# Two decoder layers with convolution, latent attention and mixture of experts on one core: router, roots, embedding matmuls, pieces loaded ahead, rotary keys and taps rearranged

## The chip, the cores and the metric

The kernel runs on one core of one Trainium2 chip, all in fp32, as one program with a hand-written order of instructions on each engine: PE (TensorE), DVE (VectorE), ACT (ScalarE), POOL (GpSimd) and SP (SyncE, which here only starts transfers). The metric is the time of one execution on the device in microseconds. Three executions of the kernel before were timed, and one more was profiled.

## The reference, cut to what matters

One inference step runs two layers for 256 prompt tokens and 8 sample tokens with the same weights. The width is 1024. Layer 0 mixes tokens by a causal convolution of 31 taps, layer 1 by latent attention with a paged cache: each of the 8 samples has 8 pages of 128 keys. Each page holds a compressed latent of 256 numbers a key and a rotary key of 32. Behind either mixer stands a mixture of 32 experts in 4 groups, and then a gated embedding.

```python
def rmsnorm(x, g):
    return x * lax.rsqrt(jnp.mean(x * x, axis=-1, keepdims=True) + EPS) * g

def conformer_conv(h, buf, w_pw1, b_pw1, w_dw, b_dw, ln_g, ln_b, w_pw2):
    u = h @ w_pw1 + b_pw1
    u = u[..., :D_CONV] * jax.nn.sigmoid(u[..., D_CONV:])
    full = jnp.concatenate([buf, u], axis=1)
    z = conv_depthwise(full, w_dw) + b_dw
    return jax.nn.silu(layernorm(z, ln_g, ln_b)) @ w_pw2, full[:, -(CONV_WIDTH - 1):]

# latent attention of the samples, keys and latents gathered by page_table
s = (einsum('bqhl,bkl->bhqk', q_lat, c_kv) + einsum('bqhr,bkr->bhqk', q_pe, k_pe)) * ATTN_SCALE
out = einsum('bhqk,bkl->bqhl', softmax(s), c_kv)

# every layer:
#   h += mixer(rmsnorm(h))
#   h += hier_moe(rmsnorm(h))
#   h += (p[i] @ W_in) * sigmoid(rmsnorm(h) @ W_gate)
```

## The kernel before, in words

**Layout.** The hidden state hT lies with the width on the partitions, in 8 chunks of 128 (KD = 8), and 264 tokens in the columns. For the choice of experts tokens lie on partitions, in three tiles of 128, 128 and 8.

**Convolution.** `expand(c)` (matmuls recorded at L483) makes one chunk of the two halves of the first projection, 8 matmuls of 128x264 for each half. DVE's `glu` and ACT's sigmoid gate it, and `shift_blocks` (L451), called by SP for two channel blocks and by ACT for the other two, copies it four times, shifted by one token each, by DMA (arena<-arena). `taps(p)` (L518 to L522, recorded at L507) convolves the chunks 2p and 2p + 1 with 128 small matmuls that use four taps at a time; DVE's `prompt_taps` (L1058) takes them out. Then follow a layer norm, pw2 with 64 matmuls of 128x264 (L483), the residual and the squares. DVE's first work is `gained` (L996), which multiplies x by a gain from the vectors.

**Router and routing.** `last_sum` (L471) ends the sum of squares over the width; the root is made on [128x264] by ACT (`root`) and DVE (`inverse_root`). `moe` (L536) begins with the router, where for each of three token tiles the tokens are the held matrix and the 36 router columns move (L544, 24 matmuls), then turns the inverse roots to columns by token (L551), makes rows of tokens by transposing (L558), multiplies the embedding `p @ W_in` (`pin`, L563 to L568, 8 chunks, of which 5 stand ahead of the count and 3 behind the ranks), and counts tokens by expert (L576) and ranks them (L582) once DVE's `route` (L1105 to L1134) has made the one-hot rows rt_M. DVE then derives a permutation of the experts by load, and windows of 64 tokens. `gather` (L602) picks tokens by one-hot matmuls.

**Experts.** Two experts make a pair. `gate_up` (L623) multiplies gate and up weights, `turn_hid` transposes, `down` (L649) multiplies the down weights, `combine` (L664) adds into hT with the gates of the tokens.

**The stream of weights.** A piece is 1 MB (128 x 2048 numbers; gate, up or down of an expert, or 1 MB of another matrix). SP issues them in the order of use into a ring of 9 slots (`NSLOT`): the slot of piece g is g mod 9, and its load waits for the last use of piece g - 9. For experts that is the whole pair's gate and up (`gate_up_done`) or down matmuls (`down_done`). `MOE_PIECES` gives the order. `expert_stream` (L1952) loads, before the permutation is known, eight ring pieces, then six pieces to places outside the ring (`ASIDE`) and the ninth ring piece. After that the number of each expert is read from the permutation (L1968), and its pieces are issued (L1942).

**Attention.** PE goes through 16 heads in a loop of 19 steps (L926 to L942). The eight samples form two batches of four, each with scores (L892), weights (L901), values (L914, L916) and output (L922). The first batch's four parts stand in steps 3, 5, 7 and 9 of the loop, the second's behind the loop. For each batch SP first reads 32 page numbers (`page_numbers`, L1923), then issues 32 transfers of cache pages (`load_cache`, L1933; 256 KB each), of which four sequences fill all buffers: those of the second batch wait for the values of the first. POOL starts the 32 key transfers of a batch (`load_kpe`, L1859; 16 KB each) in a loop of its own. After it come `so` (L949), and the output projection wo, 64 matmuls at L483.

```python
            def load_kpe(B):
                for i in range(SB):
                    with pool.Fori(0, PAGES) as n:
                        pg = pool.value_load(pages[0:1, bass.ds(n + (SB * B + i) * PAGES, 1)], min_val=0,
                                             max_val=NPOOL - 1)
                        pool.dma_start(KPT[DR * i:DR * (i + 1), bass.ds(n * PAGE, PAGE)],
```

## Time and profile before

| what | value |
|---|---|
| runs shown, median (lowest to highest) | 950.71 us (944.7 to 959.28) |
| profiled execution, its own time | 951.04 us |
| its span | 949.3 us |
| mean granted clock of PE | 0.921 |
| PE busy | 785.6 us, 83% |
| DVE, ACT, POOL busy | 34%, 22%, 6% |
| moved by DMA | 269.32 MB, 284 GB/s over the span |

The span is the time between the first and the last recorded instruction; the execution's own time is a little longer. Busy shares are means over stages that differ much: layer 0 has its convolution until about 123, pw2 until 154, the routing until 186, experts until 419 and the embedding until 453; layer 1 has attention until 610, wo until 641, routing until 670, experts until 902, then the embedding and the last norm.

### The profile page before, as it was taken

To read this page: it belongs to the slowest core of one execution; us is meant where nothing else is said; L and a number is where in the kernel's file an instruction comes from. 1 tells how busy PE (TensorE), PEld (TensorE's weight loads), DVE (VectorE), ACT (ScalarE), POOL (GpSimd) and SP (SyncE) were. 2 spreads that over 40 slices of the span, in tenths; PEclk is the share of its full clock that TensorE was granted. 3 is DMA by queue.
4 is the path that set the end of the run, shared out by engine and by line. 5 is a ranking of instruction groups with operands and counts; after the bars stand their busy time and mean duration, and the time that the engine had idled before them with its cause. 6 is when DMAs were issued, how large, how long until landed. Compare 5 with 4: busy or idle time off the path is not lost.

```text
span 949.3 us, 16693 instructions
## 1 busy us (share of the span) xinstructions
PE 785.6 (83%) x6434; PEld 569.2 (60%) x6434; DVE 321.6 (34%) x948; ACT 206.6 (22%) x490; POOL 56.2 (6%) x95
## 2 busy tenths in 40 slices
PE   5899889999777796989997685798998787878894
PEld 4767568765453464667774362587755455545683
DVE  1512333523131331255265272226232231313435
ACT  2100131621111111132135251015211110111222
POOL 3300000000000000000033232000000000000000
PEclk9989998999988988999999796799998898899997
DMA  9941826499999999974319164468699999999501
GB/s 370 368 111 51 266 76 257 164 394 408 415 417 416 415 418 415 419 317 137 129 58 348 33 222 154 164 235 314 271 401 421 414 418 417 416 415 416 220 1 46
DMA packets 59613, 269.32 MB, mean 284 GB/s; under 512 B 7312, under 2 KB 12704, under 8 KB 38416
## 3 DMA queue, kind: packets, MB, share of 16 engines
q1 hardware_dynamic: 53088, 259.31, 69.1%
q10 hardware_dynamic: 3856, 5.40, 1.9%
q0 software_dynamic: 2592, 3.54, 1.2%
q8 instruction: 53, 0.87, 0.4%
q14 instruction: 24, 0.20, 0.1%
HBM read 261.05 MB, written 2.52 MB: 278 GB/s over the span
## 4 chain that ended last, share of the span: by engine, by line
PE 49%; DMA 26%; issue 13%; POOLq 4%; DVE 4%; ACT 2%; ACTq 1%; POOL 1%; SPq 1%; DVEq 0%
DMA ring<-in_moe_w_up 22%; PE bank L623 15%; PE bank L483 13%; PE bank L602 6%; POOLq L1857 3%; PE bank L649 3%; PE bank L507 3%; PE bank L664 2%; DMA arena<-in_stateT 2%; PE bank L892 2%; DMA arena<-arena 1%; PE bank L544 1%; PE bank L558 1%; POOLq L1859 1%; POOLq L1856 1%
## 5 line engine op out<-in xcount | busy, mean ns | idle before, releaser
L623 PE MATMUL bank<-ring,arena 128*32 128x256 f32 x2048 | 148.2, 436 | 62.6 <-DMA ring<-in_moe_w_up 60.2
L623 PEld LDWEIGHTS bank<-ring,arena 128*32 128x32 f32 x2048 | 86.5, 125 | 129.9 <-issue 107.6
L483 PE MATMUL bank<-xn_sq,ring 128*128 128x264 f32 x480 | 109.8, 391 | 10.3 <-DVE xn_sq L996 10.3
L483 PE MATMUL bank<-arena,ring 128*128 128x264 f32 (+1 forms) x456 | 108.7, 399 | 6.5 <-ACT arena L1597 4.0
L483 PEld LDWEIGHTS bank<-xn_sq,ring 128*128 128x128 f32 x480 | 92.2, 193 | 27.1 <-issue 11.1
L1229 DVE TENSOR_TENSOR arena<-arena,bank 128x128 f32<-128x128 f32 x34 | 9.8, 288 | 287.7 <-ACT arena L1638 287.7
L483 PEld LDWEIGHTS bank<-arena,ring 128*128 128x128 f32 x456 | 89.8, 198 | 23.4 <-issue 7.0
L602 PEld LDWEIGHTS bank<-arena 128*128 128x128 f32 x864 | 97.9, 192 | 9.4 <-issue 9.4
L602 PE MATMUL bank<-arena 128*128 128x128 f32 (+1 forms) x864 | 101.1, 277 | 2.0 <-DVE arena L1199 2.0
L649 PE MATMUL bank<-ring,arena 128*32 128x512 f32 x512 | 65.4, 598 | 16.6 <-ACT arena L1645 16.4
L664 PE MATMUL bank<-arena 128*128 128x264 f32 (+1 forms) x288 | 70.7, 399 | 4.7 <-ACT arena L1654 4.7
L664 PEld LDWEIGHTS bank<-arena 128*128 128x128 f32 (+1 forms) x288 | 54.2, 193 | 21.3 <-ACT arena L1654 6.9
L1246 DVE TENSOR_TENSOR hT<-hT,bank 128x264 f32<-128x264 f32 x144 | 61.7, 429 | 13.5 <-PE bank L664 11.4
L1654 ACT COPY arena<-bank 64x512 f32<-64x512 f32 x68 | 39.5, 580 | 76.6 <-PE bank L649 75.8
L1638 ACT ACTIVATE arena<-bank 128x128 f32<-128x128 f32 x34 | 9.4, 278 | 165.8 <-PE bank L623 165.8
L649 PEld LDWEIGHTS bank<-ring,arena 128*32 128x32 f32 x512 | 14.9, 109 | 44.3 <-ACT arena L1645 24.3
L1859 POOL DMA_DIRECT2D arena<-in_cache_kpeT x64 | 32.1, 501 | 72.2 <-issue 72.2
L507 PE MATMUL bank<-arena 128*32 128x256 f32 x512 | 31.2, 405 | 5.8 <-DMA arena<-arena 5.8
L892 PE MATMUL bank<-arena 128*32 128x512 f32 (+1 forms) x96 | 15.6, 474 | 19.7 <-DMA arena<-in_cache_kpeT 19.7
L1569 ACT ACTIVATE xn_sq<-hT 128x264 f32<-128x264 f32 x40 | 16.1, 420 | 71.3 <-DVE hT L1000 65.7
L1630 ACT COPY arena<-bank 128x512 f32<-128x512 f32 (+1 forms) x18 | 10.1, 562 | 94.1 <-PE bank L602 94.1
L507 PEld LDWEIGHTS bank<-arena 128*32 128x32 f32 x512 | 16.9, 117 | 19.6 <-DMA arena<-arena 6.6
(243 smaller groups left out, 799.1 us busy)
## 6 DMA issues: line engine op xcount, KB each, us to landing
ring<-in_moe_w_gate SPq DMA_DIRECT2D x60, 1024.0 KB, 13.9
ring<-in_moe_w_up SPq DMA_DIRECT2D x60, 1024.0 KB, 10.8
ring<-in_moe_w_down SPq DMA_DIRECT2D x60, 1024.0 KB, 12.9
ring<-in_stream SPq DMA_DIRECT2D x35, 1024.0 KB, 14.4
ring<-in_cache_ckv SPq DMA_DIRECT2D x32, 256.0 KB, 7.4
arena<-in_moe_w_down SPq DMA_DIRECT2D x4, 1024.0 KB, 13.4
arena<-in_cache_ckv SPq DMA_DIRECT2D x16, 256.0 KB, 4.3
xn_sq<-in_cache_ckv SPq DMA_DIRECT2D x16, 256.0 KB, 6.1
```

The costliest lines, as they stand in the source:

```text
L483: t = mm(ps[:, 0:cols], lhs(k), rhs(k), start=(k == 0), stop=(k == n - 1))
L507: t = mm(ps[CG * b:CG * (b + 1), 0:TP], dg[:, c, TQ * b + q, :], shifted[p % 2][:, b, c % 2, NQ * q:NQ * q + TP], start=(q == 0), stop=(q ...
L602: t = mm(bank[k // 4][:, (k % 4) * n:(k % 4 + 1) * n], XR[:, i, k * P:(k + 1) * P], S[:, j % 2, i, 0:n], start=(i == 0), stop=(i == 2))
L623: t = mm(bank[2 + r][p0:p0 + U, 0:F].rearrange("p (c f) -> p c f", c=2), x, w[i][:, :, k * F + c * P:k * F + (c + 1) * P], start=(k == 0), ...
L649: t = mm(bank[4 + r][p0:p0 + U, :], hidT[:, r, U * (2 * i + c):U * (2 * i + c + 1)], w[i][:, c, h * 512:(h + 1) * 512], start=(c == 0), st ...
L664: mm(bank[CBANK[k % 4]][:, 0:T], O[0:n, j % 2, k * P:(k + 1) * P], gate[0:n, j % 2, :], start=True, stop=True).then_inc(s_cb, 1)
L892: t = mm(ps[HP * i:HP * (i + 1), 0:n], qlat[:, k, b, :] if k < KK else qps[:, b, :], keys, start=(k == 0), stop=(k == KK))
L1246: v.tensor_tensor(hT[:, k, :], hT[:, k, :], bank[CBANK[k % 4]][:, 0:T], ALU.add).then_inc(s_add, 1)
L1569: s.activation(sq[:, at + k, :], src[:, k, :], ACT.Square).then_inc(s_sq, 1)
L1654: s.copy(O[64 * r:64 * r + 64, j % 2, 512 * h:512 * (h + 1)], bank[4 + r][64 * h:64 * h + 64, :])\
L1857: pg = pool.value_load(pages[0:1, bass.ds(n + (SB * B + i) * PAGES, 1)], min_val=0, max_val=NPOOL - 1)
L1859: pool.dma_start(KPT[DR * i:DR * (i + 1), bass.ds(n * PAGE, PAGE)], a["cache_kpeT"][bass.ds(pg, 1)].rearrange("o p f -> p (o f)"))\
```

## The change

- **Start and other loads.** The vectors are loaded first on SP, ahead of x, instead of on ACT. The embedding inputs, router weights and router bias, which ACT issued at the start, are issued by ACT in its loop over chunks, at chunk 6. SP's shifts stand ahead of the next ring fills.
- **Taps a chunk later.** Order on PE: expand 0 to 4, taps 0, expand 5, 6, taps 1, expand 7, taps 2, means, taps 3. DVE's order follows.
- **Router.** The router weights are held and the tokens move: 8 matmuls of 36x264, six of them between the chunks of pw2 or wo, and two behind. ACT copies the logits and three matmuls transpose them.
- **Roots by token.** `token_sums` makes sums of squares by token with nine one-column matmuls, the last three squares separately; the root is then taken on [128x3] instead of [128x264], and nothing has to be turned.
- **Embedding matmuls** go from the routing to the experts' steps 3 to 6, two chunks each, into banks 6 and 7. Their weights are no piece of the ring but a load of their own behind piece 26.
- **Seventeen pieces loaded ahead**, nine in the ring and eight outside, instead of nine and six. The order at the start of `MOE_PIECES` differs.
- **Rotary keys** are issued by SP, between a batch's page numbers and its cache pages. The second sample batch stands inside the heads' loop, the first one step earlier.

```diff
-SAMPLE_AT = [3, 5, 7, 9]
+SAMPLE_AT = [[2, 4, 6, 8], [11, 13, 15, 17]]
...
-MOE_PIECES = both(0) + [(e, c) for e in (2, NSTAT) for c in range(3)]
+MOE_PIECES = both(0) + [(2, 0), (2, 1), (4, 2), (5, 2)]
...
-ASIDE = [(3, 0), (3, 1), (3, 2), (4, 2), (4, 0), (4, 1)]
+ASIDE = [(3, 0), (3, 1), (3, 2), (2, 2), (5, 0), (5, 1), (4, 0), (4, 1)]
...
+            def logits(l, norm, k):
+
+                if k == 0:
+                    open_bank(pe, ("router", l))
+                    pe.wait_ge(s_wr, 32)
+                pe.wait_ge(s_xn, KD * norm + k + 1)
+                t = mm(bank[taken["router", l][0]][0:G + E, 0:T], wr[:, l, k, :], xnT[:, k, :], start=(k == 0),
+                       stop=(k == KD - 1))
...
+            def router_tail(l, norm):
+
+                logits(l, norm, KD - 2)
+                token_sums(l, 0)
+                token_sums(l, 1)
+                logits(l, norm, KD - 1)
+                token_sums(l, 2)
+                ps = open_bank(pe, ("lg", l))
+                freed(pe, ("router", l))
+                for i, (t0, n) in enumerate(TILES):
+                    t = mm(ps[0:n, LG * i:LG * i + G + E], lgT[:, t0:t0 + n], ident[0:G + E, 0:G + E], start=True,
+                           stop=True)
...
-            for p in range(PAIRS):
-                expand(2 * p)
-                expand(2 * p + 1)
-                if p:
-                    taps(p - 1)
+            for c in range(KD):
+                expand(c)
+                if c >= 4 and c % 2 == 0:
+                    taps(c // 2 - 2)
+            taps(PAIRS - 2)
...
-            last_sum("n1")
+                if 0 < m < KD - 1:
+                    logits(0, 1, m - 1)
+            router_tail(0, 1)
...
-                pin(range(5))
...
-                pin(range(5, KD))
...
+                    if 3 <= j < 7:
+                        pin(j)
                     gate_up(b)
...
-                if i in SAMPLE_AT:
-                    (sample_scores, sample_weights, sample_values, sample_out)[SAMPLE_AT.index(i)](0)
-            sample_scores(1)
-            sample_weights(1)
-            sample_values(1)
-            sample_out(1)
+                for B in range(TS // SB):
+                    if i in SAMPLE_AT[B]:
+                        (sample_scores, sample_weights, sample_values, sample_out)[SAMPLE_AT[B].index(i)](B)
...
+            def column_root(l):
+
+                key = ("router", l)
+                ps = arrive(act, key)
+                s.copy(lgT, ps[0:G + E, 0:T]).then_inc(is_free(key), 1)
+                freed(act, ("sums", l))
+                s.activation(rcol[:], rcol[:], ACT.Sqrt).then_inc(s_rs, 1)
...
             def expert_stream(l):
 
-                for i in range(NSLOT - 1):
+                for i in range(5):
                     load_expert(l, i, MOE_PIECES[i][0])
-                arrive(sp, (("pw2" if l == 0 else "wo"), KD - 1))
-                for i in range(4):
+                arrive(sp, ("taps", KD - 1) if l == 0 else ("wo", 0))
+                for i in range(6):
                     load_aside(l, i)
+                for i in range(5, NSLOT):
+                    load_expert(l, i, MOE_PIECES[i][0])
                 arrive(sp, ("row", l, 2, 1))
-                for i in range(4, 6):
+                for i in range(6, 8):
                     load_aside(l, i)
-                load_expert(l, NSLOT - 1, MOE_PIECES[NSLOT - 1][0])
                 sp.wait_ge(s_perm, l + 1)
...
+                    if i == PIN_AT:
+                        sp.wait_ge(s_dn, NPR * l + 2)
+                        sp.wait_ge(s_gu, NPR * l + 3)
+                        sp.dma_start(aside[:, 5, :], a["pin"][l]).then_inc(s_win, 16)
+
+            sp.dma_start(vt[:], a["vectors"]).then_inc(s_vec, 16)
             sp.dma_start(hT[:], a["xT"]).then_inc(s_x, 16)
             for g in range(NSLOT):
                 fill(g)
             for p in range(PAIRS):
+                shift_blocks(sp, p, range(NQ // 2))
                 for g in range(NSLOT + 2 * p, min(NSLOT + 2 * p + 2, G_MOE0)):
                     fill(g)
-                shift_blocks(sp, p, range(NQ // 2))
...
             for B in range(TS // SB):
                 numbers = [page_numbers(SB * B + i) for i in range(SB)]
+                if B:
+                    arrive(sp, ("ss", B - 1, 1))
+                for i in range(SB):
+                    load_kpe(SB * B + i, numbers[i])
                 for i in range(SB):
                     load_cache(SB * B + i, numbers[i])
```

The new `load_kpe(b, pg)` of SP issues eight key transfers of one sample, with addresses from the page numbers already in registers.

The first place is the order of PE in the convolution, from the first half of the chunk at which the two orders part; L483 (L528 after) is the expansion, L507 (L552 after) the taps, and before it stands:

```order
L483 MATMUL bank<-xn_sq,ring 128x264 [waits bank_free0,w_in3]
L483 MATMUL bank<-xn_sq,ring 128x264 x7
L507 MATMUL bank<-arena 32x256 [waits tap_diagonals,bank_free1,shifted0]
L507 MATMUL bank<-arena 32x256 x31
L507 MATMUL bank<-arena 32x256 [waits tap_diagonals,bank_free2]
L507 MATMUL bank<-arena 32x256 x31
L483 MATMUL bank<-xn_sq,ring 128x264 [waits bank_free3,w_in4]
L483 MATMUL bank<-xn_sq,ring 128x264 x7
```

And after:

```order
L528 MATMUL bank<-xn_sq,ring 128x264 [waits bank_free0,w_in3]
L528 MATMUL bank<-xn_sq,ring 128x264 x7
L528 MATMUL bank<-xn_sq,ring 128x264 [waits bank_free1,w_in4]
L528 MATMUL bank<-xn_sq,ring 128x264 x7
L528 MATMUL bank<-xn_sq,ring 128x264 [waits bank_free2,w_in5]
L528 MATMUL bank<-xn_sq,ring 128x264 x7
L552 MATMUL bank<-arena 32x256 [waits tap_diagonals,bank_free3,shifted0]
L552 MATMUL bank<-arena 32x256 x31
L552 MATMUL bank<-arena 32x256 [waits tap_diagonals,bank_free4]
L552 MATMUL bank<-arena 32x256 x31
L528 MATMUL bank<-xn_sq,ring 128x264 [waits bank_free5,w_in4]
```

The first taps, which wait for the shifts (`shifted0`), now stand behind both halves of chunk 4 as well.

The second place is SP's order in the first expert stage, where the first pieces behind those loaded ahead are issued (a TENSOR_LOAD of permI reads an expert's number, ISA is a step on a register). Before:

```order
L1942 ISA [waits down_done]
L1942 DMA ring<-in_moe_w_gate 128x2048
L1942 DMA ring<-in_moe_w_up 128x2048 [waits gate_up_done]
L1942 DMA ring<-in_moe_w_down 128x2x1024 [waits gate_up_done]
L1942 DMA ring<-in_moe_w_down 128x2x1024 [waits down_done]
L1968 TENSOR_LOAD permI
L1968 ISA x2
L1942 ISA [waits gate_up_done]
L1942 DMA ring<-in_moe_w_gate 128x2048
L1942 DMA ring<-in_moe_w_up 128x2048 [waits gate_up_done]
```

And after:

```order
L1977 DMA ring<-in_moe_w_up 128x2048 [waits down_done]
L1977 DMA ring<-in_moe_w_down 128x2x1024 [waits down_done]
L1977 DMA ring<-in_moe_w_down 128x2x1024 [waits gate_up_done]
L2004 TENSOR_LOAD permI
L2004 ISA x2
L1977 ISA [waits gate_up_done]
L1977 DMA ring<-in_moe_w_gate 128x2048
L1977 DMA ring<-in_moe_w_up 128x2048 [waits down_done]
```

The last two rows of each are the gate and up piece of expert 8: the up piece waited for gate and up matmuls (`gate_up_done`) and now waits for down matmuls (`down_done`).

The third place is SP's order in the attention, where the page numbers (pages) of the first batch end and the transfers begin. Before:

```order
L1923 TENSOR_LOAD pages
L1923 ISA x2
L1933 ISA
L1933 DMA arena<-in_cache_ckv 128x512
L1933 ISA
L1933 DMA arena<-in_cache_ckv 128x512
```

And after:

```order
L1952 TENSOR_LOAD pages
L1952 ISA x2
L1968 ISA
L1968 DMA arena<-in_cache_kpeT 32x128
L1968 ISA
L1968 DMA arena<-in_cache_kpeT 32x128
```

After the last of 32 such key transfers the cache pages follow as before:

```order
L1968 DMA arena<-in_cache_kpeT 32x128
L1968 ISA
L1968 DMA arena<-in_cache_kpeT 32x128
L1962 ISA
L1962 DMA arena<-in_cache_ckv 128x512
L1962 ISA
L1962 DMA arena<-in_cache_ckv 128x512
```

32 transfers of keys, each with a register step, now stand between the page numbers and the first cache page.

## Rows read from the trace of the kernel before

**Rows 1.** Page, busy share by slice, in 40 slices of 23.7 us: DMA engines, then GB/s.

```profile
DMA  9941826499999999974319164468699999999501
GB/s 370 368 111 51 266 76 257 164 394 408 415 417 416 415 418 415 419 317 137 129 58 348 33 222 154 164 235 314 271 401 421 414 418 417 416 415 416 220 1 46
```

**Rows 2.** Chain of waits, first expert stage: start us, duration us, what, count.

```profile
231.63 10.70 DMA ring<-in_moe_w_up
...
377.95 11.34 DMA ring<-in_moe_w_up
```

**Rows 3.** Chain of waits, from the convolution to the first expert.

```profile
49.27 9.85 PE bank L507 x128
...
73.55 7.04 PE bank L507 x128
...
123.37 30.29 PE bank L483 x128
...
156.61 7.03 PE bank L544 x48
...
173.30 0.71 PE bank L576 x6
...
185.78 3.66 PE bank L623 x64
```

**Rows 4.** Chain of waits, attention and second routing.

```profile
525.80 1.92 DMA arena<-in_cache_kpeT
...
586.25 7.60 PE bank L892 x48
...
610.28 30.45 PE bank L483 x128
...
643.68 4.11 PE bank L544 x48
...
669.80 3.66 PE bank L623 x64
```

**Rows 5.** Timeline of PE, 48 to 50: start, us, instruction, [idle before <-releaser].

```profile
49.27 1.08 PE L507 MATMUL bank<-arena 128*32 128x256 f32 x8 [4.89 <-DMA arena<-arena]
```

**Rows 6.** Windows: a:b us, PE PEld DVE ACT POOL busy (count), PEclk, DMA share, GB/s.

```profile
54.00:55.00 1.00, 1.00 (x16) 0.50 (x12) 0.00 (x0) 0.00 (x0) 0.00 (x0) 0.57 1.06 216
158.00:159.00 1.00, 1.00 (x7) 1.00 (x6) 1.00 (x1) 0.00 (x0) 0.00 (x0) 0.50 1.02 426
220.00:226.00 6.00, 5.41 (x49) 5.17 (x47) 3.46 (x11) 0.70 (x3) 0.00 (x0) 1.00 0.94 359
```

**Rows 7.** Timeline of DVE, at the start and at the first choice of experts.

```profile
9.85 2.22 DVE L996 TENSOR_SCALAR xn_sq<-hT,vt 128x264 f32<-128x264 f32 x8 [9.85 <-DMA vt<-in_vectors]
...
169.87 0.26 DVE L1134 TENSOR_TENSOR rt_M<-rt_M 128x96 f32<-128x96 f32 x1
```

**Rows 8.** Page, DMA issues: out<-in, count, KB each, us to landing.

```profile
hT<-in_xT SPq DMA_DIRECT2D x1, 1056.0 KB, 6.1
```

**Rows 9.** Timeline of SP's DMA issues, first expert stage.

```profile
189.65 0.36 SPq L1942 DMA_DIRECT2D ring<-in_moe_w_gate  x1
...
216.50 0.34 SPq L1942 DMA_DIRECT2D ring<-in_moe_w_gate  x1
```

**Rows 10.** By line of SP's instructions: duration ns min/median/max, first to last start us.

```profile
L1923 SPq TENSOR_LOAD <-pages x64: 260/266/517, 479.3 to 532.2; - x64
...
L1933 SPq DMA_DIRECT2D arena<-in_cache_ckv x16: 345/346/369, 496.9 to 557.1; - x16
...
L451 SPq DMA_DIRECT2D arena<-arena x32: 627/628/1346, 32.6 to 102.3; - x32
```

**Rows 11.** Timeline of SP's cache page issues, both batches.

```profile
496.91 4.46 SPq L1933 DMA_DIRECT2D arena<-in_cache_ckv  x8
...
553.42 4.06 SPq L1933 DMA_DIRECT2D arena<-in_cache_ckv  x8
```

**Rows 12.** Tile of the cache pages: time from issue to landing.

```profile
DMA to landing us min/median/max: 2.6/6.2/9.9
```

250 lines of the change are left out of this document (129 added, 121 removed).

## The prediction

> **What bounds the kernel now.** I read the slices of the page first [rows 1]: the DMA engines stand at 9 in slices 9 to 17 and 30 to 37, the two expert stages, where they move 400 GB/s and more. There the weights' transfers set the time. Between them lie the convolution, two routing stages and the attention, with DMA mostly under 7. Then I followed the chain of waits. In the expert stage it is made of weight pieces that land, at 242.33 and at 389.29, 58 pieces apart [rows 2]: 2.53 us for a piece of 1 MB. In the convolution and the routing it stays on PE: taps, pw2 from 123.37, router from 156.61, count at 173.30, first expert matmul at 185.78 [rows 3]. In the attention it passes through the rotary keys' DMAs; the first batch's last one lands at 527.72 and PE starts its scores behind it at 527.96, those of the second batch at 586.25 [rows 4]. So there are six terms: what PE loses in the convolution and in each routing, how long each expert stage transfers, and when the attention's inputs land.
>
> **Convolution, -8.8 us.** PE waits 4.89 us for shifted taps before 49.27 [rows 5], and the 128 matmuls of this first pair of tap chunks take 9.85, against 7.04 for the same work at 73.55 [rows 3]. The granted clock in 54 to 55 is 0.57 with PE fully busy [rows 6]. After the change two more expansion halves (16 matmuls of 264 columns, 0.47 us each by the 64 of pw2 in 30.29 [rows 3], so 7.5 us) stand where PE waited. That covers the 4.89, and PE no longer comes to the taps out of a pause: 9.85 - 7.04 = 2.8 more. Later, tap and expansion work only change places on a PE that is busy either way; I cost that at nothing, and if a shift were late there it would be below 1 us. The start: DVE's first gained chunk waits for the vectors until 9.85 [rows 7]. They now go first on SP. x lands 6.1 us behind its issue [rows 8], which is in the first microsecond, so near 7.0, and near 7.5 with 50 KB of vectors ahead; the first weight piece follows x, at the latest 1 MB later, 2.8 us at the 370 GB/s of the first slice [rows 1]. I take 8.7, between the two: 1.1, with ends 0 and 2.3. The router's loads move later and remain hidden: they are due behind 150. Sum -4.9 - 2.8 - 1.1 = -8.8; ends -6.5 and -10.
>
> **First routing, -4.8 us.** Before, pw2's start to the first expert matmul is 185.78 - 123.37 = 62.41 [rows 3]. After, step by step. pw2 itself is 30.29, and 6 router matmuls between its chunks at 0.47 make 2.8. From pw2's end (153.66) to the one-hot rows (169.87 + 0.26 = 170.13, [rows 7]) it was 16.47. Out go the 48 narrow router matmuls, 7.03 [rows 3]; in come two wide ones, 0.95; roots on 128x3 instead of 128x264 save some 0.8 of DVE and ACT. That leaves 9.6. The count stood at 173.30, 3.2 behind its input, because PE had embedding matmuls ahead of it; they are gone, and 0.4 is left for the hand-over. Count to first expert matmul stays 12.48. Then the clock. Without the embedding matmuls PE has almost nothing while DVE chooses experts. Before, the pause of 3 us ahead of 156.61 was followed by a granted 0.50 with PE at 1.00 busy [rows 6]. For the gather and the first gate and up I take a loss of 2 us (0 to 6, the upper end being half of the 12.48). 30.29 + 2.8 + 9.6 + 0.4 + 12.48 + 2 = 57.6, so -4.8; ends -0.8 and -6.8.
>
> The Trainium skill, page "TensorE: Matmul & The Clock Gate", section "Why this matters for your kernels", says that idle gaps in the middle of a kernel give the fast clock back. It speaks against taking the embedding matmuls out of the routing. Rows 6 agree as far as they go (0.57 and 0.50 behind a gap). By the rule at its full price this term would be near -1 instead of -4.8.
>
> **Second routing, -1.9 us.** The same steps, but its narrow router matmuls took 4.11, not 7.03 [rows 3, 4], so 2.9 less is saved. From wo's start to the first expert matmul it was 59.52 [rows 4]. Ends +2 and -4.
>
> **Expert stages, +3.2 us each.** Seventeen pieces instead of fifteen are loaded ahead, and the embedding weights join behind them as a load of their own: one piece less in the stream, -2.5 at 2.53 a piece. What the embedding matmuls cost PE inside the experts lies beside transfers: PE waits there for pieces, of which single ones take 10.7 and 11.3 us to land [rows 2]. Against this stands the ring. From SP's first issue behind the permutation, 189.65, to the one that waits for the third pair's down matmuls, 216.50, it is 26.85 us [rows 9]. Before, pieces 9 to 19 of the order are issued in that time, 11 pieces or 27.9 us of data: the DMA engines stay at work, and the rate only dips to 359 GB/s in 220 to 226 [rows 6], where slices 10 to 16 have 408 to 418 [rows 1]. After, the ninth slot holds the down piece of expert 4, and piece 17, the up piece of expert 8 that reuses it, waits for those same down matmuls (the second place shown with the change). Only pieces 9 to 16 go out ahead, 8 or 20.3 us of data. The engines run dry for 26.85 - 20.3 = 6.6, against a dip worth about 1 before: +5.7. -2.5 + 5.7 = +3.2 for each layer. Ends -2.5 (no hole, if PE is earlier against the stream) and +4.
>
> **Attention, +13.4 us, the largest term.** Before, SP reads the first batch's 32 page numbers from 479.3 on [rows 10] and issues its cache pages from 496.91 [rows 11]: 17.6 us for 32, 0.55 each. Eight pages took 4.46 to issue, 0.56 each, though the DMA instruction itself is 0.346 [rows 10, 11]. POOL issues the keys beside this, by itself. After, SP issues 32 key transfers between numbers and pages (third place). No row shows a key's DMA on SP. From both sides: at worst 0.65, as the tap shifts with their 0.628 [rows 10]; at best 0.40, the bare 0.346 and small register steps, nothing overlapped. I take 0.55, the pitch of the cache pages, since that is the same instruction with a register in its address. Then the pages start at 496.9 + 17.6 = 514.5 and their issue ends at 532.1. A page lands 6.2 us behind its issue [rows 12], so the first scores begin at 538.2, not 527.96: +10.2. The products of the first batch end 25.3 us later as before (527.96 to 553.3; the issue at 553.42 waits for them, [rows 11]), at 563.5. SP meanwhile reads numbers (532.1 + 17.5 = 549.6), issues keys (567.2), then pages (584.8); the last lands at 591, where before the second scores began at 586.25: +4.7. From there to wo it was 610.28 - 586.25 = 24.0, batch two alone on PE. After, the batch stands inside the heads' loop, with a head between its steps, as the first batch did: 25.3 for its four steps, and 7.4 for the heads and outputs that remain behind. wo starts at 591 + 25.3 + 7.4 = 623.7, so +13.4. Per 0.1 us of key issue this moves by 8.8: with 0.40 it is near +4.6 (the second batch is then bound by other waits), with 0.65 it is +22.2. POOL is out of the path.
>
> The Trainium skill, page "DMA: Bandwidth & Descriptors", section "Issuing engines are not separate DMA queues", says that starting DMAs on several engines saves only sequencer time, usually small beside the transfer. The rows here disagree for small transfers: a key of 16 KB is 0.04 us of data at some 400 GB/s, and an issue on SP takes 0.55. By the rule the attention term would be about 0; the first rival has that as a mechanism of this kernel.
>
> **The sum.** The profiled execution took 951.04 us, its span is 949.3, and 1.7 lies around it; the runs' median is 950.71, so nothing is corrected. 951.04 - 8.8 - 4.8 + 3.2 + 13.4 - 1.9 + 3.2 = 955.3. I forecast 955 us, +0.5%. A measurement of this kernel can tell about 2% from no change: bounds 932 and 970.
>
> **The rivals.**
> One, faster: key issues on SP cost nothing that ends last. For it: SP idles before 479.3 and its order alone keeps the pages late; if it gets to the keys earlier than I think, or the heads between the steps cover the delay, attention comes to 0. With it go no hole in the stream (-2.5 twice), no clock loss (-6.8 and -3.9) and -9.9 in the convolution: 951.0 - 9.9 - 6.8 - 3.9 - 5 = 925. Against: the reads start with the stage, and the pages stand behind the keys in SP's order. Chance 0.16.
> Two: no hole in the stream, all else as forecast. 955.3 - 2 x 5.7 = 944. For it: the third pair's down may come earlier than 26.85, as more of its pieces are there beforehand. Chance 0.15.
> Three, slower: a key's issue on SP costs 0.65, as a shift's does. The place is SP's order before each batch's pages; attention +22.2, total 964. It passes 970 from 0.72 us a key on. For it: the key writes 32 partitions, a different form than the page. Against: the register steps are the same. Chance 0.20, of it beyond 970 0.12.
> Four: the change does not do what it says in the convolution; the shifts come equally late against the taps, since SP and ACT issue them in the same sequence, and only the start gains. 955.3 + 7.7 = 963. Against: the shifts now stand ahead of the ring's fills. Chance 0.05.
> The forecast itself has 0.44, with a range of its own of 946 to 963.
>
> **How the numbers follow.** Faster than 932 is rival one and the low tail of two, 0.20. Slower than 970 is rival three's tail and a sum of bad ends, 0.14. In between 0.66. The range of 931 to 970 leaves some 0.2 outside.
>
> **What would show it.** In the changed kernel's profile: no wait of PE for a shift, and a first pair of tap chunks of 7 us; pw2's start to the first expert matmul 57.6; some 6 us without transfers 21 to 27 us behind the first ring issue in each expert stage; 17.6 us of key issues on SP before each batch's pages; first scores 10 us later against the first page number than before; PE at a lower clock behind the routings. The forecast is wrong if the scores start where they did, if wo starts less than 5 us later against the first page number, if the stream shows no hole, or if the embedding matmuls show up as waits in the experts.

## The result, and the profile after

The changed kernel takes 969.89 us (median of 4 runs, 966.58 to 972.65) against 950.17 for the kernel before: a ratio of 1.0233, 95% interval 1.0183 to 1.0284. It is slower by 2.3%, where 0.5% and no measurable change were forecast; the interval leaves open whether it is a little more or a little less than 2%. The profiled execution took 966.58 us with a span of 964.6, the lowest of the four; against the one before (span 949.3) that is 15.3 us. The medians differ by 19.7 us; the other 4 us of it stand in no trace.

The chain of waits of the changed kernel, the rows that answer to [rows 3, 4] (start us, duration us, what, count; L528 is the old L483, L552 the taps L507, L490 the router, L621 the gather, L642 the first expert line, L927 the sample scores):

```profile
53.52 7.04 PE bank L552 x128
60.56 14.44 PE bank L528 x64
...
101.70 8.80 PE bank L552 x128
...
121.83 9.09 PE bank L528 x32
130.92 0.56 PE bank L490 x2
131.49 3.76 PE bank L528 x16
...
166.60 0.94 PE bank L597 x6
...
173.70 7.48 PE bank L621 x48
...
181.90 3.66 PE bank L642 x64
...
592.54 7.95 PE bank L927 x69
...
624.22 9.07 PE bank L528 x32
...
668.97 1.05 PE bank L597 x6
...
683.65 3.66 PE bank L642 x64
```

From such rows, and from the timeline of PE for the ends of the expert stages, one gets the stages, each from the start of its first PE work to that of the next:

| stage | before | after | forecast | measured |
|---|---|---|---|---|
| start to pw2 | 123.4 | 121.8 | -8.8 | -1.5 |
| pw2 to first expert matmul | 62.4 | 60.1 | -4.8 | -2.3 |
| experts, layer 0 | 231.1 | 234.0 | +3.2 | +3.0 |
| embedding and query inputs | 62.2 | 63.3 | 0 | +1.1 |
| attention, to wo | 131.2 | 145.0 | +13.4 | +13.8 |
| wo to first expert matmul | 59.5 | 59.4 | -1.9 | -0.1 |
| experts, layer 1 | 231.8 | 235.2 | +3.2 | +3.4 |
| embedding, last norm | 47.7 | 45.7 | 0 | -2.0 |

The two large costs, attention and expert stages, came near their forecast. What failed are the gains: 15.5 us were forecast and 3.9 came. The timeline of PE shows the convolution's part (start, us, instruction, [idle before <-releaser]):

```profile
11.09 6.83 PE L528 MATMUL bank<-xn_sq,ring 128*128 128x264 f32 x16 [11.09 <-DMA ring<-in_stream]
...
101.70 8.80 PE L552 MATMUL bank<-arena 128*32 128x256 f32 x128 [3.32 <-DMA arena<-arena]
```

PE starts 0.7 later than before (11.09 against 10.35) and needs 6.83 us for its first 16 matmul records (5.55 before). The first taps at 53.52 wait for nothing and take 7.04, as forecast; but the last ones now wait 3.32 us and take 8.80. Before, they had this row:

```profile
104.93 7.11 PE L507 MATMUL bank<-arena 128*32 128x256 f32 x128 [0.87 <-DMA arena<-arena]
```

In the middle of the changed kernel's last taps the granted clock is about half (windows, in the form of [rows 6]):

```profile
104.00:106.00 2.00, 2.00 (x25) 0.97 (x20) 0.00 (x0) 0.00 (x0) 0.00 (x0) 0.51 1.03 434
```

SP's issues in the first expert stage, and the windows around them (a:b us; busy time of PE, PEld, DVE, ACT, POOL; clock; DMA share; GB/s):

```profile
185.80 0.42 SPq L1977 DMA_DIRECT2D ring<-in_moe_w_down  x1
...
195.70 0.34 SPq L1977 DMA_DIRECT2D ring<-in_moe_w_gate  x1
212.47 0.34 SPq L1977 DMA_DIRECT2D ring<-in_moe_w_up  x1
```

```profile
190.00:206.00 16.00, 15.27 (x205) 10.64 (x197) 3.86 (x12) 3.35 (x7) 0.00 (x0) 1.00 1.02 410
206.00:214.00 8.00, 7.64 (x77) 4.73 (x73) 3.72 (x9) 1.71 (x4) 0.00 (x0) 1.00 0.39 127
214.00:230.00 16.00, 15.21 (x176) 10.94 (x169) 5.72 (x17) 2.47 (x6) 0.00 (x0) 1.00 0.98 407
```

Against [rows 9]: between a gate piece at 195.70 and its up piece at 212.47 SP issues nothing, and from 206 to 214 the DMA engines are busy for 39% of the time. That is the hole. It was forecast as 6.6 us, 5.7 more than before; 61% of 8 us is 4.9, and summed in windows of 2 us the missing share is 5.4 us, against 0.3 in the dip before. The forecast's frame was right too: 26.67 us pass from the first issue at 185.80 to the one at 212.47 (26.85 forecast), with 8 pieces ahead of the wait.

SP in the attention, against [rows 11]; then the key transfers by line (duration ns min/median/max):

```profile
497.36 16.17 SPq L1968 DMA_DIRECT2D arena<-in_cache_kpeT  x32
513.71 3.97 SPq L1962 DMA_DIRECT2D arena<-in_cache_ckv  x8
...
549.12 16.87 SPq L1968 DMA_DIRECT2D arena<-in_cache_kpeT  x32
566.17 4.54 SPq L1962 DMA_DIRECT2D arena<-in_cache_ckv  x8
```

```profile
L1968 SPq DMA_DIRECT2D arena<-in_cache_kpeT x64: 315/316/1421, 497.4 to 565.7; - x64
```

32 key issues in 16.17 us are 0.505 each, where 0.55 was taken. The pages start at 513.71; 514.5 was forecast. What PE's scores wait for has changed with it. The timeline of PE at the first scores, of the kernel before and then of the changed kernel:

```profile
527.96 1.03 PE L892 MATMUL bank<-arena 128*32 128x512 f32 x1 [10.99 <-DMA arena<-in_cache_kpeT]
```

```profile
539.67 1.03 PE L927 MATMUL bank<-arena 128*32 128x512 f32 x1 [24.82 <-DMA ring<-in_cache_ckv]
```

Before, the keys end last: POOL's loop issues one each 1.5 us (32 from 478.55 to 525.80). After, the cache pages behind the keys on SP end last.

### The profile page after: what moved, and what is told of

Same layout as the page of the kernel before. It is cut to its first block, busy times and chain, and to the rows that moved or that the text cites. A ratio compares the mean times of both kernels' runs of the same rounds, so it can differ in the third digit from the quotient of the medians.

```text
span 964.6 us, 16235 instructions
## 1 busy us (share of the span) xinstructions
PE 784.6 (81%) x6398; PEld 564.8 (59%) x6398; DVE 316.0 (33%) x946; ACT 207.6 (22%) x492; POOL 24.1 (3%) x32
## 4 chain that ended last, share of the span: by engine, by line
PE 57%; DMA 25%; SPq 8%; issue 4%; DVE 4%; ACT 1%; ACTq 1%; DVEq 0%
DMA ring<-in_moe_w_up 22%; PE bank L528 20%; PE bank L642 14%; PE bank L621 6%; SPq L1952 3%; SPq L1962 3%; PE bank L668 3%; PE bank L697 3%; SPq L1968 3%; PE bank L552 2%; PE bank L473 1%; DMA ring<-in_stream 1%; PE bank L490 1%; DMA ring<-in_cache_ckv 1%; PE bank L927 1%
## 5 line engine op out<-in xcount | busy, mean ns | idle before, releaser
L642 PE MATMUL bank<-ring,arena 128*32 128x256 f32 x1984 | 135.9, 426 | 59.9 <-DMA ring<-in_moe_w_up 57.5
L642 PEld LDWEIGHTS bank<-ring,arena 128*32 128x32 f32 x1984 | 82.6, 122 | 118.5 <-issue 94.8
L528 PE MATMUL bank<-xn_sq,ring 128*128 128x264 f32 x480 | 111.1, 394 | 11.1 <-DMA ring<-in_stream 11.1
L528 PE MATMUL bank<-arena,ring 128*128 128x264 f32 (+1 forms) x456 | 112.3, 403 | 6.5 <-ACT arena L1642 4.0
L621 PE MATMUL bank<-arena 128*128 128x128 f32 (+1 forms) x864 | 104.9, 283 | 7.2 <-DVE arena L1238 7.2
L621 PEld LDWEIGHTS bank<-arena 128*128 128x128 f32 x864 | 101.6, 198 | 14.0 <-issue 14.0
L528 PEld LDWEIGHTS bank<-xn_sq,ring 128*128 128x128 f32 x480 | 93.0, 194 | 28.3 <-issue 11.9
L528 PEld LDWEIGHTS bank<-arena,ring 128*128 128x128 f32 x456 | 89.0, 198 | 28.3 <-issue 12.1
L668 PE MATMUL bank<-ring,arena 128*32 128x512 f32 x512 | 61.7, 598 | 15.9 <-ACT arena L1685 15.7
L927 PE MATMUL bank<-arena 128*32 128x512 f32 (+1 forms) x96 | 15.0, 452 | 40.4 <-DMA ring<-in_cache_ckv 40.4
L668 PEld LDWEIGHTS bank<-ring,arena 128*32 128x32 f32 x512 | 14.4, 109 | 43.7 <-ACT arena L1685 23.7
L927 PEld LDWEIGHTS bank<-arena 128*32 128x32 f32 x96 | 4.2, 124 | 51.0 <-issue 51.0
L552 PE MATMUL bank<-arena 128*32 128x256 f32 x512 | 30.1, 396 | 3.3 <-DMA arena<-arena 3.3
L1495 DVE SCALAR_TENSOR_TENSOR arena<-bank,cst 128x384 f32<-128x384 f32 x16 | 8.8, 553 | 69.5 <-PE bank L883 69.5
L1670 ACT COPY arena<-bank 128x512 f32<-128x512 f32 (+1 forms) x18 | 10.1, 562 | 98.9 <-PE bank L621 98.9
## 6 DMA issues: line engine op xcount, KB each, us to landing
ring<-in_moe_w_down SPq DMA_DIRECT2D x60, 1024.0 KB, 13.4
```

Of the source, the lines that this page charges most:

```text
L528: t = mm(ps[:, 0:cols], lhs(k), rhs(k), start=(k == 0), stop=(k == n - 1))
L552: t = mm(ps[CG * b:CG * (b + 1), 0:TP], dg[:, c, TQ * b + q, :], shifted[p % 2][:, b, c % 2, NQ * q:NQ * q + TP], start=(q == 0), stop=(q ...
L621: t = mm(bank[k // 4][:, (k % 4) * n:(k % 4 + 1) * n], XR[:, i, k * P:(k + 1) * P], S[:, j % 2, i, 0:n], start=(i == 0), stop=(i == 2))
L642: t = mm(bank[2 + r][p0:p0 + U, 0:F].rearrange("p (c f) -> p c f", c=2), x, w[i][:, :, k * F + c * P:k * F + (c + 1) * P], start=(k == 0), ...
L668: t = mm(bank[4 + r][p0:p0 + U, :], hidT[:, r, U * (2 * i + c):U * (2 * i + c + 1)], w[i][:, c, h * 512:(h + 1) * 512], start=(c == 0), st ...
L927: t = mm(ps[HP * i:HP * (i + 1), 0:n], qlat[:, k, b, :] if k < KK else qps[:, b, :], keys, start=(k == 0), stop=(k == KK))
```

## The experiments

Every run was timed in 3 to 5 rounds beside the kernel before on its own chip; ratios are to that kernel. Stages are read from one profiled execution of each, and "attention" is counted in its own stage, from its first query matmul, so that earlier stages do not enter.

### a1 and a2: what the attention pays for

Keys back on POOL (`load_kpe` of the kernel before), all else as changed:

```diff
-                for i in range(SB):
-                    load_kpe(SB * B + i, numbers[i])
...
+            load_kpe(0)
...
+            arrive(pool, ("ss", 0, 1))
+            load_kpe(1)
```

> The changed kernel, but POOL issues the rotary keys again as in the kernel before; the second sample batch stays inside the heads' loop. Theory (two parts): the key issues on SP delay the first scores by 10 us, and the place of the second batch costs about 8 us of its own because heads stay behind it. Then the first scores return to 528 from 538, the second scores to 586, but wo starts at 586 + 25.3 + 7.4 = 619, 5 us earlier than the changed kernel's 624.2, and the total is 962 to 965. Rival: the key issues on SP are the whole loss; then wo starts at 610 and the total is 953 to 956.

Second batch behind the loop, keys on SP (the orders of DVE and ACT go back with it):

```diff
-SAMPLE_AT = [[2, 4, 6, 8], [11, 13, 15, 17]]
+SAMPLE_AT = [[3, 5, 7, 9]]
...
+            sample_scores(1)
+            sample_weights(1)
+            sample_values(1)
+            sample_out(1)
```

> The changed kernel, but the four parts of the second sample batch stand behind the heads' loop again, and the first batch's in steps 3, 5, 7 and 9. The keys stay on SP. Theory (two parts): the second scores start at 592 as in the changed kernel, then 24.0 us to wo as in the kernel before: wo at 616 to 617, 8 us earlier than 624.2, total near 960. Rival (the key issues are the whole loss, the place is free): wo stays at 624 and the total at 967 to 970.

Measured: a1 965.41 us, ratio 1.0167 (1.0110 to 1.0224); a2 958.80 us, ratio 1.0118 (1.0052 to 1.0183). The chain of waits of a1, then of a2:

```profile
535.04 6.95 PE bank L927 x48
...
592.40 7.40 PE bank L927 x69
...
624.09 8.79 PE bank L528 x32
```

```profile
591.86 7.26 PE bank L927 x48
...
615.55 9.08 PE bank L528 x32
```

The attention stage begins at 485.06 in a1 and at 477.44 in a2 (479.07 before, 479.25 after). Second scores behind that start: before 107.2, a1 107.3, after 113.3, a2 114.4 us. From them to wo: before 24.0, a2 23.7, after 31.7, a1 31.7. So the two causes are separate and add up: keys on SP cost 6 to 7 us, and the second batch inside the loop costs 7.7 to 8, because heads stay behind it: PE waits 15.55 us ahead of the second scores in the changed kernel, 8.70 before, and does those heads afterwards. The rival of both runs, that the keys are the whole loss and the place is free, falls. Both theories were right in size. The totals of single runs are noisier than these differences: a1's stages ahead of the attention alone were 5.8 us longer than those of the changed kernel.

### a3: the hole in the stream

```diff
-MOE_PIECES = both(0) + [(2, 0), (2, 1), (4, 2), (5, 2)]
+MOE_PIECES = both(0) + [(2, 0), (2, 1), (2, 2), (5, 2)]
...
-ASIDE = [(3, 0), (3, 1), (3, 2), (2, 2), (5, 0), (5, 1), (4, 0), (4, 1)]
+ASIDE = [(3, 0), (3, 1), (3, 2), (4, 2), (5, 0), (5, 1), (4, 0), (4, 1)]
```

> The changed kernel, but the ninth ring slot holds the down piece of expert 2 (freed one pair earlier) and the down piece of expert 4 lies outside the ring in its place. Theory (the hole is SP waiting behind that slot): one piece more, nine instead of eight, goes out before the third pair's down matmuls, the time without transfers shrinks from 6.6 to about 4 us, and each expert stage shortens by 2.5 us, from 234.0 and 235.3 to 231.5 and 232.8 (first expert matmul to the embedding's first), total 5 us less. Rival (the number loaded ahead and the embedding matmuls set the stage's length, not the hole): both stages stay within 0.5 us.

Measured: 962.68 us, ratio 1.0136 (1.0076 to 1.0197). SP's issues in its first expert stage:

```profile
194.98 0.59 SPq L1977 DMA_DIRECT2D ring<-in_moe_w_gate  x1
202.16 0.34 SPq L1977 DMA_DIRECT2D ring<-in_moe_w_up  x1
211.90 0.33 SPq L1977 DMA_DIRECT2D ring<-in_moe_w_gate  x1
```

One piece more goes out, at 202.16, before the wait that ends at 211.90, as the theory has it. Summing the missing DMA share in windows of 2 us gives a hole of 5.4 us for the changed kernel and 3.4 for a3 in layer 0, 6.2 and 3.7 in layer 1. So the slot makes the hole. What the hole costs is another matter. The stage of layer 0 did not shorten (234.0 to 234.6), and that of layer 1 went from 235.2 to 233.3, where 2.5 us each were expected. Over the eight profiled kernels that keep the changed kernel's stream, the same stages take 234.0 to 236.2 and 233.6 to 235.7; with the edit they take 234.6 and 233.3 here and 234.4 and 233.2 in c3. By the means that is 0.5 and 1.7 us less, and in layer 1 only 0.3 below b3 and c1, which lack the edit. In both layers of a3 PE's last wait for weights ends 194.9 and 194.8 us behind the first expert matmul, and the 39.7 and 38.5 us behind it are PE's own work. Neither theory nor rival is decided: in layer 0 a hole 2 us smaller shortens the stage by nothing that the scatter would show, in layer 1 perhaps by most of what it lost.

### a4 and b1: what made the first taps wait

The old order of taps in the changed kernel (DVE's order goes back with it):

```diff
-            for c in range(KD):
-                expand(c)
-                if c >= 4 and c % 2 == 0:
-                    taps(c // 2 - 2)
-            taps(PAIRS - 2)
+            for p in range(PAIRS):
+                expand(2 * p)
+                expand(2 * p + 1)
+                if p:
+                    taps(p - 1)
```

> The changed kernel, but taps in the order of the kernel before on PE and DVE. Theory: the first taps wait 4 to 5 us again at half clock (9.9 instead of 7.1 us), and the wait of 3.3 us before the last taps stays, since it comes from the expert pieces that share the DMA engines with the last shifts; pw2 starts at 129, 7 us later than the changed kernel's 121.8. Rival (the new order itself makes the last shifts late, as only taps 2 and half of the means stand between): the last wait falls to 1 us or less with full clock, and pw2 starts at 125.

Measured: 968.56 us, ratio 1.0196 (1.0114 to 1.0277). The timeline of PE:

```profile
46.04 7.12 PE L552 MATMUL bank<-arena 128*32 128x256 f32 x128
...
101.61 8.80 PE L552 MATMUL bank<-arena 128*32 128x256 f32 x128 [3.51 <-DMA arena<-arena]
```

Neither theory nor rival had this: the first taps start at 46.04 without any wait and at full clock though no chunk was put ahead of them, and pw2 starts at 121.75, where the changed kernel has 121.83. Taps a chunk later adds nothing here; what it would do without the rest of the change was not run. The other half of the theory came: the last wait stays at 3.51, so it is not the new order that makes the last shifts late. What removed the 4.89 us was another line of the change, and b1 puts it alone into the kernel before:

```diff
             for p in range(PAIRS):
+                shift_blocks(sp, p, range(NQ // 2))
                 for g in range(NSLOT + 2 * p, min(NSLOT + 2 * p + 2, G_MOE0)):
                     fill(g)
-                shift_blocks(sp, p, range(NQ // 2))
```

> The kernel before with one part of the change alone: SP issues the shifts of a chunk pair ahead of the next two ring fills; taps keep their old place. Theory (the run with the old order of taps had no wait at the first taps, so the ring fills ahead of the shifts were what delayed them): the wait of 4.9 us and the half clock at the first taps go, and as the last shifts are issued at the same distance from the expert pieces as before, the last wait stays below 1 us; pw2 starts at 123.4 - 4.9 - 2.7 = 115.8 and the total falls by 7 us. Rival (something else of the change removed the wait, the loads moved off ACT's start): the first taps wait 4.9 us as before and pw2 starts at 123.

Measured: 943.85 us, ratio 0.9924 (0.9877 to 0.9970). The timeline of PE of b1:

```profile
44.78 7.11 PE L507 MATMUL bank<-arena 128*32 128x256 f32 x128 [0.34 <-DMA arena<-arena]
...
97.84 7.11 PE L507 MATMUL bank<-arena 128*32 128x256 f32 x128 [1.01 <-DMA arena<-arena]
```

The wait is down from 4.89 to 0.34, the taps take 7.11, pw2 starts at 116.28, 7.1 us earlier. The theory is confirmed and the rival falls: two ring fills of 1 MB that SP issued ahead of the shifts held them back (the chain's transfer of 11.50 us that ended at 49.22 before).

### b2: what makes the last taps wait

```diff
+            sp.wait_ge(s_u4[1], 16 * NQ * NQ * 2)
             expert_stream(0)
```

> The changed kernel, but SP issues the first expert pieces only when all shifts of the last chunk pair have landed. Theory (the pieces issued at 97.8, in the middle of ACT's last shifts, make these land 2 to 2.5 us later): the wait before the last taps falls from 3.3 to about 1 us and the taps run at full clock (7.1 instead of 8.8), pw2 starts 4 us earlier, near 118; the expert stage does not change. Rival (ACT issues the shifts late by itself): the wait stays at 3 us.

Measured: 966.73 us, ratio 1.0135 (1.0094 to 1.0176). The last taps wait 1.67 us and run at 7.11, and pw2 starts at 117.58, 4.2 us earlier. The span of this execution does not show it (966.2 against 964.6), as its expert stage took 236.1 us instead of 234.0, just inside what other variants show, and its routing 61.4 instead of 60.1; the ratio is lower than the changed kernel's 1.0233. The chain's last shift (ACT issues it) tells why. The changed kernel:

```profile
97.48 4.18 DMA arena<-arena
```

The kernel b2:

```profile
96.86 2.23 DMA arena<-arena
```

All 14 profiled kernels give one table of it, with the time from ACT's last shift issue to SP's first expert piece, and from that shift's issue to its landing:

| piece behind the last shift's issue by | kernels | the shift lands after |
|---|---|---|
| -0.32 to +0.03 us | a1, a2 | 5.54, 3.25 us |
| 0.28 to 0.35 | changed, a3, a4, b3, b4, c2 | 3.73 to 4.21 |
| 0.39 to 0.62 | before, c1, b1 | 2.35 to 2.51 |
| held back | b2, c3, d1 | 2.14 to 2.42 |

So it was no property of the new order: the last shift lands late where a piece is issued within a third of a microsecond of it or ahead of it. That the pieces are the cause is shown by holding them back (4.18 to 2.23 us from the changed kernel to b2, 4.01 to 2.42 from b4 to d1). Before stood just on the good side (0.39), the changed kernel on the bad one (0.29). Each is one execution, so the bounds themselves are rough.

### b3: the order on SP

```diff
-            for g in range(G_PG0, G_MOE1 - 1):
+            for g in range(G_PG0, G_MOE1 - 4):
                 fill(g)
             sp.wait_ge(s_pg, 16)
+            early = [page_numbers(i) for i in range(SB)]
+            for g in range(G_MOE1 - 4, G_MOE1 - 1):
+                fill(g)
```

> The changed kernel, but SP reads the first batch's 32 page numbers ahead of its last three ring fills of the first layer, where it waits for a slot anyway. Theory (SP's serial order of numbers, keys and pages is what the scores wait for): the first key goes out at 479.5 instead of 497.4, the first scores start 17 us earlier, near 522, the first batch's values with them, the second batch's start moves from 592.5 to about 575, and wo starts 15 to 17 us earlier than 624.2, near 608; total 951 to 955. Rival (the transfers themselves, 8 MB a batch, or heads on PE set the start): the first scores start less than 8 us earlier.

Measured: 948.29 us, ratio 0.9988 (0.9954 to 1.0021), not to be told from the kernel before. SP's issues of b3:

```profile
478.31 17.25 SPq L1968 DMA_DIRECT2D arena<-in_cache_kpeT  x32
495.74 3.99 SPq L1962 DMA_DIRECT2D arena<-in_cache_ckv  x8
...
530.80 16.86 SPq L1968 DMA_DIRECT2D arena<-in_cache_kpeT  x32
547.84 4.36 SPq L1962 DMA_DIRECT2D arena<-in_cache_ckv  x8
```

And its first scores on PE:

```profile
521.11 1.03 PE L927 MATMUL bank<-arena 128*32 128x512 f32 x1 [7.60 <-DMA ring<-in_cache_ckv]
```

The keys start at 478.31 instead of 497.36, the first scores at 521.11 instead of 539.67, wo at 605.44. The attention stage fell from 145.0 to 127.5 us. Reading 32 page numbers costs SP 17.5 us, and it had that time free while it waited for ring slots. Transfers or heads were not the limit; the rival falls.

### b4 and d1: versions that beat both

b4 is the kernel before with the edits of b1 and b3 and with the keys issued by SP (`load_kpe` of the change); router, sample batches and stream stay.

> The kernel before with three edits: shifts ahead of the ring fills, keys issued by SP, and the first batch's page numbers read ahead of the last three ring fills; sample batches, stream, router and embedding stay as before. Theory: convolution -7.6; the first scores at 520 instead of 528 (on the scale of the kernel before) as pages and keys are complete sooner than POOL's loop was; the second scores 573 instead of 586, then 24 us to wo: -13. Total about 930, 2% under the kernel before. Rival: PE's heads are in the way of the second batch, attention gains 5 us or less, total 938 or more.

Measured: 934.11 us, ratio 0.9802 (0.9743 to 0.9862). Its chain of waits in the attention:

```profile
568.80 7.78 PE bank L892 x48
...
593.01 28.76 PE bank L483 x128
```

wo starts at 593.01, 120.4 us behind the start of the stage, 10.8 less than before (13 expected). Two things differ from the kernel before: POOL's loop of 1.5 us a key is gone, and the page numbers no longer stand ahead of the transfers. Early page numbers with the keys left on POOL were not run. The last shift was on the bad side (PE waits 2.99 us), so d1 adds the line of b2:

> The kernel with three edits to the one before (shifts ahead of ring fills, keys issued by SP, early page numbers), and a fourth: SP issues the first expert pieces only when all shifts of the last chunk pair have landed. Theory (the last shift lands 2.1 to 2.5 us behind its issue where no piece is issued within 0.35 us of it, 4 to 5.5 us where one is): the last wait is 0.7 to 1.7 us and never 3, pw2 starts near 116, and the total is 930 to 934, at most 3 us under the three edits. Rival (holding the first pieces back makes the first expert stage longer, as it was 2 us longer in the changed kernel with this edit alone): first expert matmul to the embedding's first takes 234 instead of 231 to 232 and nothing is won, total 934 to 937.

Measured: 932.60 us, ratio 0.9816 (0.9775 to 0.9857). The last wait is 1.14, pw2 starts at 116.89, and the first expert stage takes 230.0, so holding the pieces back did not make it longer, and the rival falls. By their intervals d1 and b4 are the same; both beat both kernels.

### c1: the clock behind the routing

```diff
                 ps = open_bank(pe, ("cnt", l))
+                for i in range(4):
+                    mm(ps[:, 0:T], ones, cst[:, 0:T], start=True, stop=True)
...
                 for b in range(8):
                     pe.wait_ge(free[b], used[b])
+                for i in range(6):
+                    mm(bank[7][:, 0:T], ones, cst[:, 0:T], start=True, stop=True)
```

> The changed kernel, with matmuls of 128x264 that compute nothing needed in PE's two pauses of each routing: four ahead of the token counts (1.9 us) and six behind the ranks (2.8 us). Theory (the gather runs at half clock since the embedding matmuls are gone from before it): with PE busy through the pause the gather takes 5.6 us instead of 7.5 in both layers, and the first expert matmul comes 1 to 2 us earlier in each; total -2 to -4. Rival (the clock there is not set by the pause): the gather stays at 7.4 to 8.3 as in all variants of the changed kernel so far, and the routing gets longer by what the fillers delay.

Measured: 966.24 us, ratio 1.0184 (1.0109 to 1.0259). The timeline of PE of the changed kernel, then of c1:

```profile
173.70 7.48 PE L621 MATMUL bank<-arena 128*128 128x128 f32 x48 [3.33 <-DVE arena L1238]
```

```profile
166.20 5.62 PE L611 MATMUL bank<-cst 128*128 128x264 f32 x12 [2.58 <-DVE rt_em L1206]
171.61 5.67 PE L625 MATMUL bank<-arena 128*128 128x128 f32 x48
```

And the windows of the changed kernel in its gather, then of c1:

```profile
174.00:176.00 2.00, 2.00 (x11) 2.00 (x11) 1.72 (x13) 0.15 (x1) 0.00 (x0) 0.50 0.00 0
```

```profile
172.00:174.00 2.00, 2.00 (x21) 2.00 (x19) 0.00 (x0) 0.00 (x0) 0.00 (x0) 1.00 0.00 0
```

With PE busy ahead of it the gather takes 5.67 us at a granted 1.00 (2.4 GHz), without it 7.48 with 0.50 (1.2 GHz) in 174 to 176. In the first layer it was 7.35 to 8.29 in every other variant of the changed kernel without fillers and 5.61 in all four that keep the embedding matmuls in the routing. So that part of the theory holds. The other does not: the six fillers ran at the low clock themselves and took 5.6 us, so the first expert matmul came 1.6 us later against pw2, not earlier (61.6 and 61.1 us in the two layers, against 60.1 and 59.4). The granted clock was 0.50 in 166 to 170, under the fillers. Buying the clock back with empty work costs more than it returns here. The embedding matmuls of the kernel before gave the fast gather with work that has to be done anyway, though not for nothing: its count stood 3.2 us behind its input because of them.

### c2: the start

```diff
-            sp.dma_start(vt[:], a["vectors"]).then_inc(s_vec, 16)
...
+            act.dma_start(vt[:], a["vectors"]).then_inc(s_vec, 16)
```

> The changed kernel, but the vectors are loaded by ACT at their old place. Theory (x and the first weight piece, issued by SP 0.45 us earlier, are what the start waits for, and the vectors arrive in time): the first matmul starts at 10.4 instead of 11.1 as in the kernel before. Rival (the first weight piece lands late for another reason, the missing router loads included): it stays at 11.1. In either case the total moves by less than 1 us, which no time can tell, only the profile.

Measured: 965.38 us, ratio 1.0173 (1.0087 to 1.0259). The first matmul starts at 10.25, against 11.09 of the changed kernel and 11.0 to 11.3 in all others that load the vectors on SP. The time is as expected, the reason only in part. In the changed kernel DVE starts at 7.25 instead of 9.85, but the first weight piece lands only at 11.0, and it, not the vectors, ends last. In c2 it is the other way round: the vectors arrive only for DVE's start at 9.74, and PE follows that.

### c3: the change with all of it mended

c3 has the edits of a2, a3, b2, b3 and c1 together.

> The changed kernel with five edits together: page numbers of the first batch early, second sample batch behind the loop, expert pieces behind the last shifts, ninth ring slot freed earlier, fillers in the routings. By what each did alone against the changed kernel (attention -17.4 and -6.9, convolution -4, stream -2 in one layer, routing -2 if the fillers work) it would be 933 to 940. Theory (the gains add): 933 to 940, level with the kernel before with three edits (934). Rival (the heads on PE take the place of the two attention gains together): attention keeps 127 us and the total stays above 941.

Measured: 938.72 us, ratio 0.9898 (0.9812 to 0.9985). The gains in the attention add: from its start to wo it is 597.29 - 477.00 = 120.3 us, as in b4, and the rival falls. pw2 starts at 116.17. The fillers cost here too: the routings take 62.1 and 61.7 us, 2 more than in the changed kernel, and the expert stages 234.4 and 233.2. It stays 1% behind b4 by the ratios, with intervals that overlap.

## Why the prediction was wrong, point by point

Of the 11 us between the 4.3 forecast and the 15.5 measured, 7.3 come from the convolution and 4.3 from the two routings; all other terms together come to -0.5.

**Convolution: -8.8 forecast, -1.5 measured. This is the step that failed.** Its three errors:

- "That covers the 4.89, and PE no longer comes to the taps out of a pause": the 4.9 and the 2.7 us were won, but not by the chunk put ahead. a4 takes the chunk away and keeps the gain; b1 has the gain from SP's order alone. I had the moved shifts in hand as an argument in the fourth rival and did not ask what they do by themselves.
- "Later, tap and expansion work only change places on a PE that is busy either way; I cost that at nothing, and if a shift were late there it would be below 1 us": the last wait grew from 0.87 to 3.32 and the taps behind it from 7.11 to 8.80 (clock 0.51 in 104 to 106), 4.1 us in all. The shift was late because expert pieces are issued at nearly the same moment.
- "I take 8.7, between the two: 1.1": the first matmul came 0.7 later instead of 1.1 earlier. x was there at 7.25, near its forecast of 7.5, but the first weight piece, which was to land by 10.3 at the latest, landed at 11.0, 9.16 us behind its issue, and ended last. All nine kernels with the vectors first on SP start at 11.0 to 11.3, the others at 10.1 to 10.5. The first 16 records took 1.3 longer besides; these nine kernels take 5.19 to 6.83 us for them, so that is within the scatter.

In numbers: -4.9 - 2.7 + 2.4 + 1.7 + 0.7 + 1.3 = -1.5, of which the 1.3 is within the scatter.

**First routing: -4.8 forecast, -2.3 measured.** The tail behind pw2 was right: from pw2's end to the count 9.74, 10.0 forecast. Wrong was the price of the router matmuls between the chunks: 0.57 us instead of 0.47, and a pw2 chunk beside one takes 3.76 instead of the 3.61 of 64 records in 14.44 (the expansion's rows in the chain). pw2 with its six router matmuls takes 35.0, and 33.1 was forecast; some 0.4 of that lies in its first two chunks. From the count to the first expert matmul it is 15.30 against 14.5; the clock, taken at 2, is 1.9 in the gather (7.48 against 5.61). The rule of the Trainium skill, page "TensorE: Matmul & The Clock Gate", section "Why this matters for your kernels", was right in kind, as c1 shows; its full price, a routing that gains about 1, was too high for this execution.

**Second routing: -1.9 forecast, -0.1 measured**, for the same reason: wo with its router matmuls takes 35.0, not 33.3.

The two routings also show a weakness that the forecast did not price. The 48 narrow router matmuls took 7.03 us in the first layer and 4.11 in the second, and from that one execution the two terms were made 2.9 apart. In b4 it is the other way round, 4.11 and 7.50, and its routings take 59.5 and 62.5 us. Both routings together take 121.4 to 122.1 us in the four kernels with the old routing and 119.1 to 122.8 in the eight with the new one and no fillers, so by the means the new routing gains about 1 us in the two layers, where 6.7 was forecast.

**Expert stages: +3.2 each forecast, +3.0 and +3.4 measured.** The hole came as told, down to the piece that SP waits with, and a3 shows that the slot makes it. That the hole is what lengthens the stages is not shown: with 2.0 and 2.5 us of it gone, the first layer's stage took 234.6, inside what it takes without that edit, and the second's 233.3, 0.3 below it. The -2.5 for one piece less was not tested either. So the number may be right by luck, and the cause of the 3 us stays open.

**Attention: +13.4 forecast, +13.8 measured.** The mechanism was right, and a1 and a2 show it. That the sum is so near is part luck: the price of a key was 0.505, not 0.55, but the last page of the second batch landed 8.50 us behind its issue where 6.2 was taken. By parts: 6 from the keys on SP (the sum had 4.7) and 7.7 from the place of the second batch (8.7, of which the 7.4 for heads and outputs was read from no row). b3 adds that what counts is SP's whole serial order, of which the 17.5 us of page numbers were as large a part as the keys. The Trainium skill, page "DMA: Bandwidth & Descriptors", section "Issuing engines are not separate DMA queues", says that several issuing engines save only sequencer time, usually small beside the transfer. Here that time is 16 us of issue before each batch for 0.5 MB of keys, while a key lands in a few us (1.7 to 5.8 before) and its data are 0.04 us at 400 GB/s.

**What was costed at nothing.** The embedding stages moved by +1.1 and -2.0 us. In both, a few matmuls behind a pause ran at the lower clock in one execution and not in the other (1.22 and 1.08 us for records that take 0.61 to 0.7). No run tests that, and I leave it as a difference of single executions.

**The range and the rivals.** Rival three, slower through SP's order, was nearest to what came, but by luck, as the key was cheaper than forecast and not dearer: what came were lost gains of 11.6 us on top of the forecast costs. Its sum is also wrong. By the prediction's own steps 0.1 us more a key puts 32 issues later twice, 6.4 us and not 8.8, so 0.65 gives 962 and not 964, and 970 is passed at 0.78 us. And the chances leave 0.34 outside 932 to 970, not some 0.2. A mishap in several gains at once was not among my cases beyond a tail.

## What to carry to other kernels

Before a stall is credited to a reordering of the engine that waits, look at what else the change moves ahead of the transfer it waits for: here one line on the issuing engine gave all of it, and the reordering added nothing. An engine that issues many small register-addressed transfers is a serial resource: count its issues and number loads (here about half a microsecond each on SP, 1.5 us a key in POOL's loop), and move those that need nothing, as page numbers, into its idle waits. Work that could run while a transfer is awaited should stand ahead of the wait: moved behind it, as the heads here, it hides nothing and is paid in full. And a forecast that comes out right is not yet a cause: the expert stages' number fitted, and the run that shrank the hole did not clearly shorten them.

## What the runs showed of the hardware that was not expected

- A shift of 71 KB landed 2.1 to 2.5 us behind its issue where a 1 MB piece on another engine's queue was issued 0.39 us or more behind it or held back, and 3.3 to 5.5 where it was issued within 0.35 us of it or ahead (14 executions).
- PE idle for 3 us and matmuls behind it at half clock cost more than the pause: 2.4 us of later landing became 4.1 us in the convolution. In b4, with 2.99 us of wait before the same taps, they took 7.11 at a granted 1.00. In the same way the narrow router matmuls of the kernel before ran at a granted 0.50 in the first layer and 1.00 in the second, behind the same code. What makes the difference stays open.
- A router matmul with 36 held columns takes 0.57 us, where one of 128 takes 0.45 to 0.47, and the chunk of eight full ones behind it takes 3.76 instead of 3.61.
